# Alternating the products of two token tiles between their two PSUM banks in a float32 transformer kernel

## What is computed

```python
def swiglu(x, w_gate_up, w_down):
    g, u = jnp.split(x @ w_gate_up, 2, axis=-1)
    return (jax.nn.silu(g) * u) @ w_down
...
    for i in range(DEPTH):                       # DEPTH = 2
        h = h + 0.5 * swiglu(rms_norm(h, ffa_norm[i]), ffa_w_gate_up[i], ffa_w_down[i])
        h = h + mixer(rms_norm(h, mix_norm[i]))  # i = 0: window and latent attention; 1: forgetting attention
        h = h + 0.5 * swiglu(rms_norm(h, ffb_norm[i]), ffb_w_gate_up[i], ffb_w_down[i])
        gate = jax.nn.sigmoid(rms_norm(h, ple_norm[i]) @ ple_w_gate[i])
        h = h + gate * (p[i] @ ple_w_proj[i])
...
# experts, per token: top 16 of 128 x 128 sums of sub-key scores in each of 8 heads
        a = jax.nn.gelu(jnp.einsum("td,thkd->thk", xc, w_down[e]))
        return jnp.einsum("thk,thkd->td", g * a, w_up[e])
```

## Time and profile before

| | us |
|---|---|
| median of three runs | 2409.23 |
| lowest and highest of them | 2407.68, 2411.26 |
| the profiled execution | 2408.0 |
| its span, first to last instruction | 2405.9 |
| PE, DVE and ACT busy in the span | 2257.1, 1375.7, 1064.7 |

### The profile page before, as it was taken

How to read it: one execution, slowest core, us unless ns; L and a number is a source line. 1 busy time by engine, 2 the same in 40 slices (tenths; PEclk the granted TensorE clock), 3 DMA queues, 4 the chain that set the end, 5 groups by cost and what they waited for, 6 DMA issues and landing times.

```text
span 2405.9 us, 27190 instructions
## 1 busy us (share of the span) xinstructions
PE 2257.1 (94%) x11226; PEld 1901.8 (79%) x11226; DVE 1375.7 (57%) x1811; ACT 1064.7 (44%) x1249; POOL 76.6 (3%) x51
## 2 busy tenths in 40 slices
PE   7999799999999999999999874999999999999997
PEld 6887678877887778877777754988888899888885
DVE  4455755455555655456665598645555565555553
ACT  5445644454444554445654542234444422444442
POOL 1000000000000000001000240000000000000000
PEclk9999899999999999999999995589999965999998
DMA  7555145544554335545444330034454410544551
GB/s 257 179 190 187 40 162 192 189 176 162 184 183 165 115 112 190 182 177 188 154 144 175 116 130 1 1 140 180 177 203 177 176 68 27 187 180 175 199 187 70
DMA packets 51658, 366.70 MB, mean 152 GB/s; under 512 B 5872, under 2 KB 6016, under 8 KB 7760
## 3 DMA queue, kind: packets, MB, share of 16 engines
q1 hardware_dynamic: 50208, 359.38, 41.3%
q0 software_dynamic: 1328, 5.58, 0.7%
HBM read 363.90 MB, written 1.05 MB: 152 GB/s over the span
## 4 chain that ended last, share of the span: by engine, by line
PE 71%; issue 16%; DVE 8%; ACT 4%; POOL 0%; DMA 0%; DVEq 0%; POOLq 0%; SPq 0%; ACTq 0%
PE bank L252 20%; PE bank L254 19%; PE bank L253 19%; PE bank L1769 8%; PE bank L257 3%; DVE w_lo L242 1%; ACT w_hi L237 1%; ACT x_hi L279 1%; DVE arena L1696 1%; PE bank L715 1%; PE bank L693 1%; DVE arena L1693 1%; DVE arena L1714 1%; DVE stat L756 1%; DVE one_j L753 1%
## 5 line engine op out<-in xcount | busy, mean ns | idle before, releaser
L242 DVE TENSOR_TENSOR w_lo<-raw,w_hi 128x2048 fp32r<-128x2048 f32 x330 | 753.8, 2291 | 578.5 <-ACT w_hi L237 578.4
L237 ACT ACTIVATE w_hi<-raw 128x2048 fp32r<-128x2048 f32 x340 | 649.9, 1911 | 315.2 <-PE bank L254 301.0
L252 PE MATMUL bank<-w_hi,x_hi 128*128 128x512 f32 (+1 forms) x1756 | 698.5, 398 | 33.3 <-DVE x_lo L288 12.8
L254 PE MATMUL bank<-w_hi,x_lo 128*128 128x512 f32 (+1 forms) x1756 | 686.9, 391 | 0.0
L253 PE MATMUL bank<-w_lo,x_hi 128*128 128x512 f32 (+1 forms) x1756 | 686.6, 391 | 0.0
L252 PEld LDWEIGHTS bank<-w_hi,x_hi 128*128 128x128 f32 x1756 | 333.2, 190 | 103.6 <-ACT x_hi L279 16.4
L252 PE MATMUL bank<-w_hi,a_hi 128*128 128x512 f32 x960 | 376.7, 392 | 16.9 <-ACT a_hi L441 10.2
L254 PEld LDWEIGHTS bank<-w_hi,x_lo 128*128 128x128 f32 x1756 | 332.7, 189 | 70.0
L253 PEld LDWEIGHTS bank<-w_lo,x_hi 128*128 128x128 f32 x1756 | 333.6, 190 | 65.0
L254 PE MATMUL bank<-w_hi,a_lo 128*128 128x512 f32 x960 | 375.7, 391 | 0.0
L253 PE MATMUL bank<-w_lo,a_hi 128*128 128x512 f32 x960 | 375.5, 391 | 0.0
(11 more groups left out here) (179 smaller groups left out, 1373.4 us busy)
## 6 DMA issues: line engine op xcount, KB each, us to landing
raw<-in_w SPq DMA_DIRECT2D x340, 1024.0 KB, 4.8
h<-in_x SPq DMA_DIRECT2D x2, 512.0 KB, 4.9
one_i<-in_alibi POOLq DMA_DIRECT2D x1, 1024.0 KB, 5.3
arena<-in_mem POOLq DMA_DIRECT2D x1, 1024.0 KB, 5.4
arena<-in_subkeys POOLq DMA_DIRECT2D x1, 1024.0 KB, 5.4
out<-h SPq DMA_DIRECT2D x1, 1024.0 KB, 4.0
consts_sb<-in_consts SPq DMA_DIRECT2D x1, 608.0 KB, 10.0
arena<-in_p POOLq DMA_DIRECT2D x2, 256.0 KB, 2.9
```

The costliest lines, as they stand in the source:

```text
L237: act.activation(w_hi[:, u % RING, :, :], raw[:, u % RING, :, :], ACT.Copy).then_inc(*act_done.mark("w_hi", u))
L242: e.tensor_tensor(w_lo[:, u % RING, :, :], raw[:, u % RING, :, :], f32(w_hi[:, u % RING, :, :]), ALU.subtract).then_inc(*lo_by(u).mark("w_ ...
L252: pe.matmul(out, hi, w_hi[:, s, b, 0:width], start=start, stop=False)
L254: return pe.matmul(out, lo, w_hi[:, s, b, 0:width], start=False, stop=stop)
```

## The change

`product` takes a list of tiles with their banks in place of one bank, and writes each of the three kinds of matmul for all tiles of the list before the next kind. `tensor_unit` and `tensor_up` give it both tiles, so that their banks alternate from one matmul to the next; where other work stands between the tiles (`between`, the first unit of a stage) they still do tile 0, the other work, and tile 1. `tensor_down` gives it both tiles too. The marks of both tiles come with the last two matmuls of a unit. `tensor_up` waits for both banks to be free before the first matmul of a unit that has `free`.

```diff
-        def product(pe, out, s, b, width, hi, lo, start, stop):
-
-            pe.matmul(out, hi, w_hi[:, s, b, 0:width], start=start, stop=False)
-            pe.matmul(out, hi, w_lo[:, s, b, 0:width], start=False, stop=False)
-            return pe.matmul(out, lo, w_hi[:, s, b, 0:width], start=False, stop=stop)
+        def product(pe, outs, s, b, width, hi, lo, start, stop):
+
+
+            w = slice(0, width)
+            for t, out in outs:
+                pe.matmul(out, hi(t), w_hi[:, s, b, w], start=start, stop=False)
+            for t, out in outs:
+                pe.matmul(out, hi(t), w_lo[:, s, b, w], start=False, stop=False)
+            return [pe.matmul(out, lo(t), w_hi[:, s, b, w], start=False, stop=stop) for t, out in outs]
...
-            for t in range(NT):
-                if t == 1 and between:
+            outs = [(t, bank[pair[t]][:, 0:width]) for t in range(NT)]
+            for tiles in ([outs[:1], outs[1:]] if between else [outs]):
+                if between and tiles[0][0] == 1:
                     between()
                 for k in ks:
-                    if ready and t == 0:
+                    if ready and tiles[0][0] == 0:
                         ready(k)
...
-                for t in range(NT):
+                for tiles in ([outs[:1], outs[1:]] if i == 0 and between else [outs]):
                     if i == 0 and free:
-                        free(t)
-                    if i == 0 and t == 1 and between:
+                        free(0)
+                        free(1)
+                    if i == 0 and between and tiles[0][0] == 1:
                         between()
```

More of the change, by code:

```diff
@@ L248, in take, with tile @@
             return u % RING
-        def product(pe, out, s, b, width, hi, lo, start, stop):
-            pe.matmul(out, hi, w_hi[:, s, b, 0:width], start=start, stop=False)
-            pe.matmul(out, hi, w_lo[:, s, b, 0:width], start=False, stop=False)
-            return pe.matmul(out, lo, w_hi[:, s, b, 0:width], start=False, stop=stop)
+        def product(pe, outs, s, b, width, hi, lo, start, stop):
[5 more added lines that the diff above has]
+            return [pe.matmul(out, lo(t), w_hi[:, s, b, w], start=False, stop=stop) for t, out in outs]
+        def tile(operand, k):
+            return lambda t: operand(k)[:, t * P:(t + 1) * P]
         def transpose_to(pe, out, src):
@@ L356, in tensor_unit @@
             s = u % RING
-            for t in range(NT):
-                if t == 1 and between:
+            outs = [(t, bank[pair[t]][:, 0:width]) for t in range(NT)]
+            for tiles in ([outs[:1], outs[1:]] if between else [outs]):
+                if between and tiles[0][0] == 1:
                     between()
                 for k in ks:
-                    if ready and t == 0:
+                    if ready and tiles[0][0] == 0:
                         ready(k)
-                    last = product(pe, bank[pair[t]][:, 0:width], s, base + k - ks[0], width, hi(k)[:, t * P:(t + 1) * P],
-                                   lo(k)[:, t * P:(t + 1) * P], k == 0, k == chunks - 1)
-                last.then_inc(*pe_done.mark("unit", u, t))
-                if name:
-                    pe_done.also("block", *name, t)
+                    lasts = product(pe, tiles, s, base + k - ks[0], width, tile(hi, k), tile(lo, k), k == 0, k == chunks - 1)
+                for (t, _), last in zip(tiles, lasts):
+                    last.then_inc(*pe_done.mark("unit", u, t))
+                    if name:
+                        pe_done.also("block", *name, t)
             pe_done.also("used", u)
@@ L397, in tensor_up @@
         def tensor_up(pe, key, c, u, between=None, ready=None, meanwhile=None, free=None):
+            hi, lo = x_at()
+            outs = [(t, bank[GU[t]][:, :]) for t in range(NT)]
             for i in range(2):
                 s = take(pe, u + i)
-                for t in range(NT):
+                for tiles in ([outs[:1], outs[1:]] if i == 0 and between else [outs]):
                     if i == 0 and free:
-                        free(t)
-                    if i == 0 and t == 1 and between:
+                        free(0)
+                        free(1)
+                    if i == 0 and between and tiles[0][0] == 1:
                         between()
-                    for k in range(UB):
-                        kk = i * UB + k
-                        if ready and t == 0:
-                            ready(kk)
-                        last = product(pe, bank[GU[t]][:, :], s, k, BLK, x_hi[:, kk, t * P:(t + 1) * P],
-                                       x_lo[:, kk, t * P:(t + 1) * P], kk == 0, kk == KC - 1)
-                    last.then_inc(*pe_done.mark("unit", u + i, t))
-                    if i == 1:
-                        pe_done.also("up", key, c, t)
+                    for k in range(i * UB, i * UB + UB):
+                        if ready and tiles[0][0] == 0:
+                            ready(k)
+                        lasts = product(pe, tiles, s, k - i * UB, BLK, tile(hi, k), tile(lo, k), k == 0, k == KC - 1)
+                    for (t, _), last in zip(tiles, lasts):
+                        last.then_inc(*pe_done.mark("unit", u + i, t))
+                        if i == 1:
+                            pe_done.also("up", key, c, t)
                 pe_done.also("used", u + i)
@@ L423, in tensor_down @@
                 for half in range(2):
+                    outs = [(t, bank[2 * t + half][:, :]) for t in range(NT)]
                     for f in (2 * i, 2 * i + 1):
-                        for t in range(NT):
-                            last = product(pe, bank[2 * t + half][:, :], s, 2 * (f - 2 * i) + half, BLK,
-                                           a_hi[:, f, t * P:(t + 1) * P], a_lo[:, f, t * P:(t + 1) * P],
-                                           start and f == 0, stop and f == nf - 1)
+                        hi, lo = a_at()
+                        last = product(pe, outs, s, 2 * (f - 2 * i) + half, BLK, tile(hi, f), tile(lo, f),
+                                       start and f == 0, stop and f == nf - 1)[-1]
                     last.then_inc(*pe_done.mark("down", key, c, half))
```

## The result

The changed kernel takes 2415.19 us in the median of 16 runs (2410.93 to 2418.39), the kernel before beside it 2409.20 us (16 runs, 2407.68 to 2414.04). The ratio is 1.0022, with an interval of 1.0015 to 1.0029: 6.0 us slower, where 4.6 were forecast (2413.8 us), and inside the range. The chances had 0.48 on slower and 0.47 on a difference under 0.2%, so on that question the forecast hardly chose. The profiled execution of after is one of its longer ones, 2417.2 us with a span of 2415.1.

A forecast was written before the change was run, and what follows sets the result against it. PE bounds the kernel. Spacing adds zero, joints a) to e) sum to 4.6 us, taking the profiled 2408.0 to 2412.6 us; the median, 1.2 us above, becomes 2413.8 us, range 2408.3 to 2418.8.

The forecast's parts named there:

- Part 1: Spacing of products on PE: 6,548 more bank changes cost zero, between -11 and +6 us; spacing stays 0.2267 us.
- both rivals of the spacing: Product spacing: 13 ns same-bank price vanishes, 2328 us, chance 0.05; or each change costs 5 ns, 2447 us, chance 0.03.
- a): First handover of a feed-forward, four times: PE waits for both tiles of `mid`, 0.39 us later each, 1.6 us.
- b): Gate stage after the feed-forward's handover, twice: second activation and the chain behind it move later, 0.7 us in all.
- c): First projections of the first mixer: ACT's tile-0 copies start later, queues absorb part, DVE's last copy comes 0.5 us later.
- d): Query blocks of the routing: +0.35 us each, two reach DVE, 0.7 us; the two later blocks fall under its backlog.
- e): Joints of the second block's mixer: waits behind ACT's gelu and copies grow by 0.37, 0.3, 0.15 and 0.3, 1.1 us.
- The upper bound of 6.6 us: All joints of stages: if each of the eleven cost a whole activation start of 0.6 us, 6.6 us.
- Nothing is left of the sum: Rival at the joints: later starts are taken back where DVE or the loads set the pace, 2409.2 us, chance 0.04.
- a change after every product costs more: Rival on product spacing: a bank change after every product costs 5 ns, 33 us in all, 2447 us, chance 0.03.
- The clock falls: Rival at the feed-forward handovers: longer waits bring half clock for four stretches of 6.8 us, 13.6 us, 2427 us, chance 0.06.

The follow-up runs named there:

- tile by tile at the joints: Changed kernel, with each column block's last unit and the first two chunks of every feed-forward and the experts tile by tile again; ratio 0.9999.
- late marks: Kernel before, products in its order, but tile 0's mark raised by the unit's last matmul but one and one wait for both banks; ratio 1.0012.
- banks 7 and 4: Changed kernel, with chunk 1 of each feed-forward in banks 7 (tile 0) and 4 (tile 1) in place of 4 and 5; ratio 1.0011.
- banks 7 and 5: Changed kernel, with tile 0 of each feed-forward's chunk 1 in bank 7 and tile 1 still in bank 5; ratio 1.0012.
- the two halves: Changed kernel with only up and down products alternating, ratio 0.9997; and with only the other units alternating, ratio 1.0008.
- tile by tile at the query blocks: Changed kernel, with the eight units of the query blocks in the expert routing tile by tile as before; ratio 1.0012.
- bank-7 kernel: Kernel before, with tile 0 of each feed-forward's chunk 1 in idle bank 7; ratios 0.9981 and 0.9980, medians 2406.38 and 2405.62 us.

## Why the prediction was right, step by step

**Part 1** held. A change of bank after each product cost nothing: 0.2265 us against 0.2266. That removes both rivals of the spacing. The 13 ns that the spacing has over half of its half-clock value stand as before, and have nothing to do with the bank. The kernel in which most products alternate and which takes the time of before (tile by tile at the joints) confirms it over the whole program.

**a)** 1.6 us forecast, 0.45 + 0.40 + 0.37 + 0.41 = 1.63 measured, and the cause shown by two kernels (late marks open it, banks 7 and 4 close it).

**b)** 0.7 forecast, 0.36 + 0.35 measured.

**c)** 0.5 forecast, 0.12 measured. The queues were the right ones and the times in them too long. After takes 1.82 us more to get to this stage; without that, ACT's first split starts at 230.77 us in after (forecast 231.0, before 229.97), DVE's first at 232.71 (forecast 232.95, before 231.91) and its second at 234.92 (forecast 235.2, before 234.79), and the copy at 237.12 (forecast 237.47, before 237.00). So the copies of ACT come 2.5 us later against the stage, the 1.57 us that ACT had been idle behind them take this down to 0.8, and the 0.59 us that DVE had been idle before its second split take it down to 0.12. Of the 0.35 us that the copy was put too late, 0.24 are the end of ACT's copies, and 0.11 the two splits of DVE, which follow each other at 2.20 us and not at 2.25.

**d)** 0.7 forecast, 1.38 measured. The price of one joint was right (0.35), the count wasn't: I put the third and fourth query block under DVE's backlog, and they weren't hidden there. All four shifts arrive at DVE: its instructions at 1373.05, 1393.99, 1408.22 and 1427.08 us of before come 6.78, 8.33, 8.66 and 9.02 us later in after, and 2.63, 2.99, 3.34 and 3.69 us later in the kernel where only the units outside up and down alternate, each time 0.35 more. DVE never stops for the third and the fourth block, and yet it is delayed. How, the rows of the kernel before tell (DVE and POOL):

```profile
1424.65 7.77 DVE L1714 TENSOR_TENSOR arena<-arena 128x64 f32<-128x64 f32 x8
...
1422.46 4.62 POOL L242 TENSOR_TENSOR w_lo<-raw,w_hi 128x2048 fp32r<-128x2048 f32 x1 [5.57 <-ACT w_hi L237]
1427.49 4.62 POOL L242 TENSOR_TENSOR w_lo<-raw,w_hi 128x2048 fp32r<-128x2048 f32 x1 [0.41 <-ACT w_hi L237]
```

In after the same rows are

```profile
1433.33 8.11 DVE L1724 TENSOR_TENSOR arena<-arena 128x64 f32<-128x64 f32 x8
...
1431.48 4.61 POOL L242 TENSOR_TENSOR w_lo<-raw,w_hi 128x2048 fp32r<-128x2048 f32 x1 [5.94 <-ACT w_hi L237]
1436.51 4.61 POOL L242 TENSOR_TENSOR w_lo<-raw,w_hi 128x2048 fp32r<-128x2048 f32 x1 [0.42 <-ACT w_hi L237]
```

Eight small additions of DVE take 7.77 us. Most of the eight last 0.2 us; taken singly, the first lasts 2.51 us, to 1427.16, and the sixth 4.58 us, to 1432.17, and POOL's splits end at 1427.08 and 1432.11. POOL's split waits for ACT's, and ACT's for PE to have used the slot. So DVE's backlog isn't free of PE: it stands still until POOL is done, POOL runs by PE's clock of units, and the eight additions took 0.34 us more in after. The Trainium skill's page "Perfetto Trace Analysis", section Optimizing Scalar/DVE Operations, remarks that GpSimd and DVE share a read port of the SBUF, which would explain this; no run here separates it, so it is read from the rows and not shown.

**e)** 1.1 forecast, 0.30 + 0.29 + 0.11 + 0.25 = 0.95 measured.

The errors of c), d) and e) (-0.4, +0.7, -0.15) nearly cancel, which is luck: 4.6 forecast, 4.8 in the trace. The upper bound of 6.6 us was counted for eleven joints, where the list of the prediction has thirteen and fifteen opened; none cost more than 0.45. DVE's first top-16 starts 6.8 us later than before, where some 4 were foretold: the start of the program and the half clock around 850 us came on top. Between the medians stand 6.0 us, between the means 5.5 and 3.7 in the two comparisons, 4.8 us by the number of runs of after. So the joints can account for the whole of the mean difference, and the 1.2 us above them in the first medians lie within the spread. What the clock adds or takes back in the mean these runs can't tell. What remains unaccounted runs the other way: for the kernels with late marks, banks 7 and 5, and the two halves, the means are 1.5 to 2.2 us lower than their joints, for after run again 1.1, for tile by tile at the query blocks and for banks 7 and 4 0.8. The kernel before against itself also came out 1.1 us low.

**Nothing is left of the sum** fell, **a change after every product costs more** fell. **The clock falls** was wrong in place and half right in kind. The handovers of a), with 1.46 us idle, brought no half clock in any trace. But at the query blocks, where PE is idle for 1.22 and 0.74 us a little apart (0.87 and 0.74 in the kernel before), it fell to the half in three of the six profiled executions whose joints there are open (after twice, late marks) and in none of the seven whose joints are closed, at 1.65 us a time. In a fourth of the six it fell behind the 1.68 us wait of the second block's mixer instead and cost 1.56 us. The Trainium skill's page "TensorE: Matmul & The Clock Gate", section A second HAM failure mode: psum-queue depth-cycling, ties such swings to a kernel that cycles through banks and idles briefly between groups. Here the late marks, which cycle no more than the kernel before, show the same stretch, and the steady state, which cycles at each product, stays at 1.00: so it isn't the cycling. That it is the longer waits is likely from three of six against none of seven, and not shown. Why the same waits bring it in one execution and not in another, I leave open. No run tells what differs between them; the waits read the same.

The page "Perfetto Trace Analysis" of the Trainium skill, section Matmuls, asks for groups that rotate through banks so that the emptying of one hides under the next. The runs bear that out where something waits, at 0.1 to 0.45 us a joint, and the bank-7 kernel is that advice followed at the place where it was worth most.

## What to carry to other kernels

When two groups of matmuls fill two banks, do them one after the other in the last unit before a handover; between handovers their order is free. Where a first wait for a bank opens a gap and a bank stands unused, move the next group there: that gave 4.7 to 5.1 us here, and only with groups in sequence, since interleaved groups wait for the last bank of the pair. Below about 0.2% read the joints in the traces side by side, because equal kernels came out 1 us apart in their means, and look at the granted clock of each execution before you read a median.

## What the runs showed of the hardware

Small DVE additions of some 0.2 us lasted up to 4.6 us beside a 128 x 2048 subtraction on POOL, and ended within 0.1 us of its end. Changing the PSUM bank at each 128 x 512 float32r product cost nothing (46 intervals of 0.2265 us). The first pair of products behind the handover's wait took longer to get going: 0.54 us from 340.05 to the next row but 0.45 us in a running row. Half-clock stretches of a few us come and go between executions of one kernel with the same waits, and their lengths in the records were 3.4, 6.8 and 13.7 us (8.9 or 12 at the end of the program), with 139.9 or 143.4 for the long one behind the expert routing and 95.6 for the next, at about 1942; the two profiled executions of the kernel before agree in them, and behind the start every single start of PE agrees within 0.2 us.
